# Reading the sample states undecayed in a decoder-trunk kernel, four pieces in four column groups

## The reference

```python
def step(s, inp):
    qc, kc, vc = inp
    att = jnp.einsum('bhnk,bhmk->bhnm', qc, kc) * dmask
    o = (jnp.einsum('bhnm,bhmv->bhnv', att, vc)
         + jnp.einsum('bhnk,bhkv->bhnv', qc * q_decay[..., None], s))
    s = s * s_decay[:, None, None] + jnp.einsum('bhmk,bhmv->bhkv', kc * k_decay[..., None], vc)
    return s, o
```

## Time and profile before

| | us |
|---|---|
| median of 3 runs (1199.17 to 1208.51) | 1208.26 |
| the profiled execution's own time | 1210.12 |
| its span in the trace | 1208.3 |
| TensorE busy | 990.0 (82%) |
| VectorE busy | 361.8 (30%) |
| ScalarE busy | 226.5 (19%) |
| GpSimd busy | 100.8 (8%) |
| mean granted TensorE clock | 0.942 |

### The profile page before, as it was taken

How to read it: one execution, slowest core, us unless ns; L and a number is a source line. 1 busy time by engine, 2 the same in 40 slices (tenths; PEclk the granted TensorE clock), 3 DMA queues, 4 the chain that set the end, 5 groups by cost and what they waited for, 6 DMA issues and landing times.

```text
span 1208.3 us, 16392 instructions
## 1 busy us (share of the span) xinstructions
PE 990.0 (82%) x7006; PEld 723.0 (60%) x7006; DVE 361.8 (30%) x660; ACT 226.5 (19%) x465; POOL 100.8 (8%) x122
## 2 busy tenths in 40 slices
PE   6999999999996999999999947766667666666764
PEld 5888888778764775688888825433333333333333
DVE  1201583376223333423211163211135111111113
ACT  2111213204412222243100041101010101010102
POOL 0001121000123232200000041000000000000000
PEclk9999999999998999999999978999997989988788
DMA  9764557494667989833534964999999999999992
GB/s 289 244 234 158 175 180 273 162 292 115 216 204 248 300 246 304 285 122 124 192 123 139 382 278 184 417 417 416 416 417 417 416 417 416 417 416 417 417 415 81
DMA packets 138826, 343.80 MB, mean 285 GB/s; under 512 B 7640, under 2 KB 91864, under 8 KB 122360
## 3 DMA queue, kind: packets, MB, share of 16 engines
q1 hardware_dynamic: 123136, 287.94, 63.4%
q0 software_dynamic: 14464, 52.68, 12.8%
q10 hardware_dynamic: 1152, 2.10, 0.5%
HBM read 320.46 MB, written 22.20 MB: 284 GB/s over the span
## 4 chain that ended last, share of the span: by engine, by line
PE 56%; SPq 21%; DMA 10%; DVE 7%; issue 3%; ACT 2%; POOL 1%; DVEq 0%; ACTq 0%; POOLq 0%
PE psum L912 34%; SPq L742 21%; DMA arena<-in_w_up 8%; PE psum L962 5%; PE psum L662 3%; PE psum L921 2%; PE psum L1117 2%; DMA arena<-arena 2%; PE psum L672 2%; PE psum L931 1%; PE psum L646 1%; ACT arena L1248 1%; PE psum L1105 1%; DVE arena L1584 1%; DMA arena<-in_state_ret 1%
## 5 line engine op out<-in xcount | busy, mean ns | idle before, releaser
L912 PE MATMUL psum<-arena 128*128 128x264 f32 x2048 | 475.7, 389 | 0.0
L912 PEld LDWEIGHTS psum<-arena 128*128 128x128 f32 x2048 | 388.3, 191 | 82.2 <-issue 18.6
L662 PE MATMUL psum<-arena 128*32 128x256 f32 x2048 | 146.0, 435 | 114.7 <-DMA arena<-in_w_up 114.0
L662 PEld LDWEIGHTS psum<-arena 128*32 128x32 f32 x2048 | 78.4, 122 | 175.1 <-issue 151.2
L1248 ACT ACTIVATE arena<-psum 128x264 f32<-128x264 f32 (+5 forms) x180 | 75.7, 434 | 358.6 <-PE psum L912 251.9
L1248 ACT ACTIVATE arena<-arena 128x1024 f32<-128x1024 f32 (+7 forms) x67 | 58.7, 903 | 165.1 <-DVE arena L1725 84.8
L1685 DVE SCALAR_TENSOR_TENSOR arena<-arena 128x512 f32<-128x512 f32 x64 | 52.9, 888 | 116.0 <-ACT arena L1248 100.0
L1871 DVE SCALAR_TENSOR_TENSOR arena<-arena,psum 128x128 f32<-128x128 f32 x32 | 9.2, 289 | 231.3 <-ACT arena L1460 231.3
L672 PE MATMUL psum<-arena 128*32 128x256 f32 x1024 | 66.7, 405 | 11.7 <-ACT arena L1472 11.7
L1176 PE MATMUL psum<-arena 128*128 128x264 f32 x112 | 41.9, 458 | 24.3 <-DVE arena L1883 24.3
L962 PE MATMUL psum<-arena 128*128 128x256 f32 x256 | 56.3, 380 | 3.1 <-DVE arena L1532 3.1
(11 more groups left out here) (236 smaller groups left out, 701.1 us busy)
## 6 DMA issues: line engine op xcount, KB each, us to landing
arena<-in_w_gate SPq DMA_DIRECT2D x64, 1024.0 KB, 23.1
arena<-in_w_up SPq DMA_DIRECT2D x64, 1024.0 KB, 22.6
arena<-in_w_down SPq DMA_DIRECT2D x64, 1024.0 KB, 23.0
arena<-in_w_in SPq DMA_DIRECT2D x48, 1024.0 KB, 5.3
arena<-in_state_ret POOLq DMA_DIRECT2D x16, 1024.0 KB, 6.7
out_ret_s<-arena POOLq DMA_DIRECT2D x16, 1024.0 KB, 8.5
arena<-in_w_mem_kv SPq DMA_DIRECT2D x8, 1024.0 KB, 9.6
arena<-in_cache_mem_k POOLq DMA_DIRECT2D x8, 1024.0 KB, 5.9
```

Of the source, the lines that this page charges most:

```text
L662: mm = pe.matmul(psum[32 * a:32 * a + SLOTS, bank, 0:256], tokens[:, 4 * half + k, SLOTS * j:SLOTS * (j + 1)], w[:, :, k, P * a:P * (a + 1 ...
L912: mm = pe.matmul(ps(task)[:, 0:T], w[:, k, (i % 2) * P:(i % 2 + 1) * P], rhs[:, k, :], start=k == 0, stop=k == KT - 1 and not two)
```

## The change

1. Task `so` reads the tile as it was loaded, and only `sd` after it decays and updates it. TensorE waits for the load (`st_in`) in place of the update; ScalarE's decay waits for TensorE's read (`st_read`). Gamma is applied later, and (q.k) v is added to the output (task `qk`, and a small product `vqk` after the last `vs`).
2. The four pieces of a tile go to four column groups (16 columns of weights, zero where nothing belongs) in place of two. The two halves of a head are added when the result is put in its place: `soT` is four matmuls of 32 columns with the constant `place` in place of four transposes.
3. The scores `att` of a head are listed ahead of the outputs of the head before it, with two buffers `attT`.
4. The value rows have two buffers; the row of tile `s + 2` is fetched just after the broadcast of tile `s`.

The list of the states changes from `sd 0, sd 1, so 0, sd 2, so 1, ...` to `so 0, so 1, sd 0, so 2, sd 1, ...`. GpSimd's loop keeps its text, and there are three places for tiles as before.

```diff
-        ret += [("att", h)] + [("o", h, j) for j in range(4)] + [("S", h, i) for i in range(2)]
-
-    so = [("sd", 0)]
+        ret += ([("att", h + 1)] if h + 1 < HEADS else []) + [("o", h, j) for j in range(4)]
+        ret += [("S", h, i) for i in range(2)]
+
+    so = [("so", 0)]
     for s in range(2 * NS):
-        so += ([("sd", s + 1)] if s + 1 < 2 * NS else []) + [("so", s)]
+        so += ([("so", s + 1)] if s + 1 < 2 * NS else []) + [("sd", s)]
...
             def v_broadcast(s):
-                b, hp = n_state(s)
-                if s >= 1:
-                    pool.wait_ge(v_bcast, s)
-                pool.dma_start(v_row0[0:1, :], vs_rows[b:b + 1, hp * D:(hp + 1) * D]).then_inc(v_row_in, 16)
-                pool.wait_ge(v_row_in, 16 * (s + 1))
+
+                pool.wait_ge(v_row_in[s % 2], 16 * (s // 2 + 1))
                 if s >= 2:
                     pool.wait_ge(st_updated, s - 1)
-                nc.gpsimd.partition_broadcast(vb[:, s % 2, :], v_row0[0:1, :], P).then_inc(v_bcast, 1)
+                nc.gpsimd.partition_broadcast(vb[:, s % 2, :], v_row0[:, s % 2, :], P).then_inc(v_bcast, 1)
+                if s + 2 < 2 * NS:
+                    v_row(s + 2)
...
-                    pe.wait_ge(st_updated, s + 1)
-                    for i in range(2):
-                        for h2 in range(2):
-                            h = 2 * hp + h2
-                            mm = pe.matmul(psum[32 * h:32 * h + NS, 7, :], QM[:, 2 * h + i, b, :],
-                                           st[:, s % 3, 2 * h2 + i, :],
-                                           start=b == 0 and i == 0, stop=b == NS - 1 and i == 1)
+                    pe.wait_ge(q_placed, 2)
+                    pe.wait_ge(st_in[s % 3], 16 * (s // 3 + 1))
+                    for g in range(4):
+
+                        mm = pe.matmul(psum[32 * g:32 * g + 2 * NS, 7, :], QM[:, 4 * hp + g, b, :], st[:, s % 3, g, :],
+                                       start=s == 0, stop=s == 2 * NS - 1)
...
                     act.wait_ge(st_in[s % 3], 16 * (s // 3 + 1))
+                    act.wait_ge(st_read, s + 1)
```

More of the change, by code:

```diff
@@ L83, in shape_constants @@
     valid[T - 2 * P:, 2] = 0
+    place = np.zeros((P, HEADS * NS))
+    for h in range(HEADS):
+        for i in range(2):
+            for b in range(NS):
+                place[32 * (2 * (h % 2) + i) + NS * (h // 2) + b, NS * h + b] = 1.0 - 2.0 ** (-5.0 - h)
     parts = {
         "cos": np.cos(ang), "sin": np.sin(ang), "dmask": mask.reshape(P, -1),
-        "ident": np.eye(P), "kdec": kdec.reshape(P, -1), "before": (p[:, None] < p[None, :]).astype(f), "valid": valid,
+        "ident": np.eye(P), "kdec": kdec.reshape(P, -1), "before": (p[:, None] < p[None, :]).astype(f), "valid": valid, "place": place,
         "slot": np.tile(np.arange(SLOTS), (P, 1)), "count32": np.tile(np.arange(EXPERTS), (P, 1)),
@@ L160 @@
     "cs": (TP, "k", "rows"),
-    "QM": (KT * 64, "k", "gc"),
-    "attT": (384, "rows", "gc"),
+    "QM": (KT * 2 * NS * NS, "k", "gc"),
+    "pqk": (KT * NS, "k", "rows"),
+    "qkb": (HEADS * NS, "rows", "rows"),
+    "vqk": (VT * NS, "rows", "gb"),
+    "attT": (2 * 384, "rows", "gc"),
     "oT": (VT * T, "ga", "ret"),
@@ L1095, in _ @@
                     c = h * DV + j * P
-                    pe.matmul(ps(task)[:, 0:TP], v_rows[:, 0, c:c + P], attT[:, 0:TP], start=True, stop=False)
-                    end(task, pe.matmul(ps(task)[:, P:TP], v_rows[:, 1, c:c + P], attT[:, TP:TP + P],
+                    pe.matmul(ps(task)[:, 0:TP], v_rows[:, 0, c:c + P], attT[:, h % 2, 0:TP], start=True, stop=False)
+                    end(task, pe.matmul(ps(task)[:, P:TP], v_rows[:, 1, c:c + P], attT[:, h % 2, TP:TP + P],
                                         start=False, stop=True))
@@ L1124, in _ @@
                     for j in range(4):
-                        mm = pe.transpose(ps(task)[:, j * P:(j + 1) * P], os_[:, j * P:(j + 1) * P], ident)
+                        mm = pe.matmul(ps(task)[:, 32 * j:32 * j + 32], os_[:, j * P:(j + 1) * P], k_("place"),
+                                       start=True, stop=True)
                     end(task, mm)
@@ L1350, in _ @@
                     q = task[1]
-                    run(vs_rows[0:NS, 512 * q:512 * q + 512], ps(task)[0:NS, :], ACT.Copy, free_of(task))
+                    run(vs_rows[:, 512 * q:512 * q + 512], ps(task)[0:NS, :], ACT.Copy, free_of(task))
                 elif kind == "vr":
@@ L1358, in _ @@
                     full(act, task)
+                    if task == ("ga", 0):
+                        act.wait_ge(v_qk_ready, HEADS)
                     if kind == "gb":
@@ L1642, in _ @@
                         v(V.memset(QM, 0.0))
-                        v(V.tensor_copy(diagonal(QMd, KT), qT[:, :, TP:T]))
+                        for hp in range(2):
+                            spots = QM[:, 4 * hp:4 * hp + 4].rearrange("p k b c -> p k (b c)")
+                            did(V.tensor_copy(spots[:, :, NS * hp:NS * hp + 17 * NS - 16:17],
+                                              qT[:, 4 * hp:4 * hp + 4, TP:T]), q_placed)
+                    else:
+                        v(V.tensor_tensor(pqk.rearrange("p h i b -> p (h i) b"), qT[:, :, TP:T], kT[:, :, TP:T], ALU.mult),
+                          qk_multiplied)
                 elif kind == "sl":
@@ L1689, in _ @@
                     full(dve, task)
+                    did(V.tensor_tensor(oT.rearrange("p (h j) t -> p h j t", h=HEADS)[:, :, :, TP:T],
+                                        ps(task)[:, 0:P].rearrange("p (j h b) -> p h j b", j=4, h=HEADS), vqk, ALU.add),
+                        free_of(task))
+                elif kind == "qk":
+                    full(dve, task)
+                    v(V.tensor_copy(qkb, ps(task)[:, 0:HEADS * NS].rearrange("p (h b) -> p h b", h=HEADS)), free_of(task))
+                elif task == ("vs", 3):
+                    read(dve, last["v"])
                     for h in range(HEADS):
-                        did(V.tensor_copy(oT[:, 4 * h:4 * h + 4, TP:T],
-                                          ps(task).rearrange("p (j c) -> p j c", j=4)[:, :, 32 * h:32 * h + NS]),
-                            free_of(task) if h == HEADS - 1 else None)
+                        did(V.tensor_tensor(vqk[:, h], vT[:, 4 * h:4 * h + 4, TP:T],
+                                            bc(qkb[:, h:h + 1, :], (P, 4, NS)), ALU.mult), v_qk_ready)
                 elif kind == "on":
```

39 lines of the change are left out of this document (26 added, 13 removed).

## The result

| | before | changed |
|---|---|---|
| median | 1206.78 us (4 runs, 1199.17 to 1208.51) | 1350.78 us (4 runs, 1347.38 to 1351.62) |
| profiled execution | 1210.12 us | 1347.38 us |
| span in the trace | 1208.3 us | 1345.5 us |
| mean granted clock | 0.942 | 0.899 |

The ratio is 1.119, with a 95% interval of 1.114 to 1.124: slower by 144 us, against 137 forecast.

The account below looks back on a forecast made before the run. State stage bound by TensorE and GpSimd's queue together, experts by weights. Twelve turns, 277 us, put `soT` at 655 (+136), the end adds 1: 1210.12 becomes 1347, forecast 1345 since that execution stands 1.9 above the median; range 1295 to 1390.

Parts of the forecast that it names:

- The ring: State stage: read, two tasks, decay, update, store's issue, broadcast, load, next read wait on each other without slack, once per tile.
- a turn: One pass of the ring per tile: 20.5 us with an output, plus 2.4 us for the clock; 12 turns, 277 us.
- The step's own remark: GpSimd's queue before the change: in the round from 473.35 a load, a store and a row together needed 9.5 us.
- The clock: TensorE's tasks behind each idle wait run partly at the lower clock: 2.4 us per turn, bounds 0 and 5.1.
- The cold rival: All the ring's TensorE work at the lower clock, 2.7 us more per turn: 1377; chance 0.2, shared with slow loads.
- the GpSimd round of 10.9 us: Kernel before, state stage: broadcast to next broadcast, 7.38 us of it waiting for a value row queued behind a store.
- TensorE becomes the bound: State stage: loads come in time, saving 15 us of work and up to 22 of waits: 1171; chance 0.05.

## Why the prediction was right

*Direction and mechanism.* The ring, found in the two queues and the list, is shown three ways: by the 13 waits, 136.6 us in all, by a changed list alone, and by a changed queue alone.

*The size of a turn.* Twelve turns came to 274.9 us against 277. By kind they were 24.2 to 25.1 us with a state `S` (24.2 forecast), 21.9 to 23.1 with an output (22.9), 22.5 with a projection alone (22.3) and 19.8 for tile 12 (20.6). `so 3` at 358.2 against 357; `soT` at 653.3 against 655. Part by part, in the turn from 498.76: 7.8 us from the read to the decays (7.9 forecast, clock included), 4.9 for decays and update (4.9), 0.3 to the store's issue (0.3), 2.9 to the load's issue (2.85), 6.3 to the next read (6.7, and 0.2 of handovers).

*The term that was right for a wrong reason.* I priced the broadcast and the row's issue at 2.1 us and the load at 6.7 behind them. The sum held (9.2 us from the store's issue to the read, against 9.55), but moving the load ahead of the broadcast changed nothing, while a smaller store did. The step's own remark, that a load, a store and a row together needed 9.5 us, was the better description.

*The clock.* 2.4 us per turn were taken from one place at 382 us. The changed kernel's reads took 1.91 instead of 1.05 and its first projections 4.6 to 5.8 instead of 3.83, about 2.2 in all on average. That a single place came so near the mean of twelve turns is partly luck. Keeping TensorE busy gave back 1.5 of them. The cold rival, all of the ring at the lower clock, did not come: the `o` in the turn shown takes 0.59 us, the same as in the kernel before.

*The last 7 us.* The medians differ by 144 us and the profiled executions by 137.3; the profiled execution of the changed kernel was the fastest of its four runs, and that of before, at 1210.12, lay above all its four. That is the spread between executions, and no run here says where it lies.

*What I had of the other edits.* Four groups at 0.9 us each: 0.84 measured, 13 us over the stage. The scores a head ahead I called a real gain that would be hidden. On the kernel with the new list, where nothing hides it, it is no gain. And the GpSimd round of 10.9 us, which I took as a limit beside TensorE, cost the kernel before 4 us by itself, and with it the waits for scores that I had put down to the scores' place.

*The rival on the other side.* "TensorE becomes the bound" was priced at 1171 and said to need loads that do not wait for the update of the tile. The list with the update directly behind its read gives 1180.6, without the waits. `soT` comes 28.8 us earlier than before where I had 37; 4 of the missing 8 us are a stage that starts later in that execution (its first projection at 325.6, before at 321.6), 1 is the read at 0.98 and not 0.9. The rest I did not resolve.

## What to carry to other kernels

When a read is moved ahead of an update, look at what the update releases: here the load of the tile after next, whose issue stood behind the update in another engine's queue. Write the ring down as a sum (read, tasks in between, update, store, load) and divide it by the number of tiles that the list lets run ahead; it has to stay below the bounding engine's work per tile. Here one list place was the difference between one turn per tile and one turn for two.

Before counting queue instructions on such a ring, ask what transfers beside them. A load issued behind a store of its own size in the same queue may land no earlier for being issued earlier.

## What the runs showed of the hardware

- A load of 1 MB in GpSimd's queue took 6.2 us from issue to landing when issued 2.9 us behind a store of 1 MB, 8.3 us when issued 0.8 us behind it, and 5.9 us when issued as soon behind a store of 256 KB.
- After waits of 8 to 12 us the read of 8 records took 1.91 us against 1.05. The granted clock was 0.50 in it (498.8 to 500.6 us), the lower of the two levels (1.2 GHz), 0.75 in the projection behind it, and full after that. With filler work and waits of 0.8 to 4.1 us the read mostly ran at the high clock, but in some turns the clock fell in the work behind it (the projection at 472.57, 5.51 us, after a wait of 1.8 us that had the full clock).
- Work that stands in the time of the lower clock is partly free: a read 1.7 us longer cost 0.7 us per turn.
- Four column groups against two: 0.98 and 1.82 us from the read's start to the next task's, for the same four products of 512 columns at the high clock.
